# Joined norms between experts and mixer, split products in the merge, tile-wise transposes

## The reference

```python
# first block (one layer)
h = rmsnorm(x, norm1_g); proj = h @ w_in                 # q, k, v of two attentions, two gates
ya, yb = neighbourhood_attention(...), gqa_attention(...)  # each (512, 512)
merged = sigmoid(ga) * (ya @ w_proj_a) + sigmoid(gb) * (yb @ w_proj_b)
x = x + merged @ w_out
x = x + peer(rmsnorm(x, norm2_g), w_q, sub_keys, u, v)   # 16384 experts, 8 heads, top 16
x = rmsnorm(x, norm_f_g)
# second block
h = rmsnorm(x, norm_pre); proj = h @ w_in_2
# causal convolutions, silu, chunked state scan over 16 heads, gated norm, short convolution
mix = concat([y_ssd, y_sc]) @ w_out_2
x = x + rmsnorm(mix, norm_post)
out = x + sigmoid(x @ w_ple_gate) * (p @ w_ple_proj)     # p is (512, 256)
```

## Time and profile before

| | us |
|---|---|
| median of 3 runs | 2385.95 (2381.82 to 2391.55) |
| the profiled execution | 2387.96 |
| its span, first to last instruction | 2386.2 |
| TensorE matmul busy | 2208.9 (93%) |
| VectorE, ScalarE, GpSimd busy | 1517.6, 853.3, 442.6 |
| mean granted TensorE clock | 0.968 |

### The profile page before, as it was taken

One profiled execution on the slowest core, in us unless ns is written; L12 is line 12 of the kernel. 1 busy time (PEld: TensorE's weight loads), 2 busy tenths in 40 slices (PEclk: granted clock), 3 DMA queues, 4 the chain that ended last, 5 costly groups with the idle time before them and its releaser, 6 DMA issues. The chain is left out here.

```text
span 2386.2 us, 29236 instructions
## 1 busy us (share of the span) xinstructions
PE 2208.9 (93%) x11157; PEld 1896.2 (79%) x11157; DVE 1517.6 (64%) x2683; ACT 853.3 (36%) x1419; POOL 442.6 (19%) x306
## 2 busy tenths in 40 slices
PE   7999999798999889889999999999993999989789
PEld 6777666688999888879788888999983798877567
DVE  3546323324999989855888887688886624445643
ACT  3344212222334645763333333333323332222212
POOL 0100000000122010001433333366671000013100
PEclk9999999899999999999999999999996999989899
DMA  5321223212678584668999998799984322210220
GB/s 205 110 84 54 80 106 110 84 36 76 228 249 258 174 253 136 198 217 305 381 378 376 368 378 320 265 354 340 341 284 152 106 89 89 99 43 4 82 101 36
DMA packets 211420, 450.27 MB, mean 189 GB/s; under 512 B 13776, under 2 KB 133584, under 8 KB 204496
## 3 DMA queue, kind: packets, MB, share of 16 engines
q1 hardware_dynamic: 174416, 314.16, 38.0%
q0 software_dynamic: 36864, 134.23, 15.7%
HBM read 403.51 MB, written 44.83 MB: 188 GB/s over the span
## 5 line engine op out<-in xcount | busy, mean ns | idle before, releaser
L1568 PE MATMUL bank<-Vh,Hh 128*128 128x512 f32 x768 | 299.2, 390 | 5.3 <-DVE Hl L1642 5.3
L1570 PE MATMUL bank<-Vh,Hl 128*128 128x512 f32 x768 | 299.5, 390 | 0.0
L1569 PE MATMUL bank<-Vl,Hh 128*128 128x512 f32 x768 | 299.5, 390 | 0.0
L901 PE MATMUL bank<-XH,Ue 128*128 128x384 f32 x672 | 233.2, 347 | 21.6 <-DVE Ue L890 21.6
L939 POOL DMA_INDIRECT ring<-in_v,gidx x128 | 218.6, 1708 | 161.5 <-DVE x_res L951 62.9
L1588 ACT ACTIVATE Vh<-Vr 128x1024 fp32r<-128x1024 f32 x128 | 135.8, 1061 | 303.6 <-PE bank L1570 300.1
L902 PE MATMUL bank<-XL,Ue 128*128 128x384 f32 x672 | 227.6, 339 | 0.0
L903 PE MATMUL bank<-XH,Ue 128*128 128x384 f32 x672 | 227.6, 339 | 0.0
L1637 DVE TENSOR_TENSOR Vl<-Vr,Vh 128x1024 fp32r<-128x1024 f32 x128 | 156.5, 1223 | 54.7 <-ACT Vh L1588 54.7
L939 POOL DMA_INDIRECT ring<-in_u_rows,gidx x92 | 109.8, 1194 | 405.5 <-DVE ghid L944 225.0
L1568 PEld LDWEIGHTS bank<-Vh,Hh 128*128 128x128 f32 x768 | 144.2, 188 | 36.0 <-DVE Hl L1642 7.0
(11 more groups left out here) (360 smaller groups left out, 4890.7 us busy)
## 6 DMA issues: line engine op xcount, KB each, us to landing
Vr<-in_v SPq DMA_DIRECT2D x128, 512.0 KB, 7.2
...
```

Source lines behind the costliest of these rows:

```text
L901: pe.matmul(ps, h[:, k], c.Xh[:, k, 0:DN], start=k == 0, stop=False)
L1568: pe.matmul(ps, Hh[r][:, tok], Vh[r][:, cut], start=p == 0, stop=False)
L1569: pe.matmul(ps, Hh[r][:, tok], Vl[r][:, cut], start=False, stop=False)
L1570: mm = pe.matmul(ps, Hl[r][:, tok], Vh[r][:, cut], start=False, stop=p == PK - 1)
```

## The change

- `transposes_pe` works by token tile: for tile tt it waits for that tile alone and transposes kt 0 to 3; kt 4 to 7 follow as before.
- project: squares of tiles 1 and 3 on VectorE; on both engines the halves of kt 0 to 3, weight piece 0, the halves of kt 4 to 7, pieces 1 and 2.
- merge: the attention outputs are split too (`yh`, `yl`), a third weight piece per m, 3m + 2, holds the projection weights, and L756's matmuls become split ones. Part n of the first half of `w_out` waits for 2(n + 1) merged tiles. `mT` takes the place of `a.y`.
- experts: `due` divides by `work[-LEAD]`. SP also loads `nf`. At the end, tile GT first and then each of the three others as its last matmul is done: VectorE adds the banks and multiplies by `nf` into `c.xn` (in `c.XT`), ScalarE squares both `c.X` and `c.xn`.
- phase_between is gone. mixer_in scales `c.xn` by rr = ((EPS * ss + ss2) / D + EPS^2)^-0.5, which joins both norms, and holds transposes and halves; the residual itself is scaled behind them. Blocks 2 and 3 are loaded only then. Groups 0 to 3 use banks 4 to 7, and group 0 waits k by k.
- scan: at its end the embeddings of the second half, kept in `c.ur` by ScalarE; transposes by tile. mixer_out takes them from there, and TensorE has no `embed` behind the groups.

```diff
...
 def transposes_pe(pe, c, src, n):
-    pe.wait_ge(c.scaled, SCALED[n])
-    for kt in range(KT):
-        if kt >= 4 and n in HALVES:
-            pe.wait_ge(c.xlo, HALVES[n] + kt - 3)
-        elif kt >= 4:
-            pe.wait_ge(c.out_d if kt % 2 else c.out_a, OUT[n] + kt // 2 - 1)
+    for tt in range(TT):
+        pe.wait_ge(c.scaled, SCALED[n] - TT + tt + 1)
+        for kt in range(4):
+            mm = pe.transpose(c.bank[kt][:, tt * P:(tt + 1) * P], src[:, tt, kt * P:(kt + 1) * P], c.ident)
+            if tt == TT - 1:
+                mm.then_inc(c.turned, 1)
+    for kt in range(4, KT):
+        pe.wait_ge(c.xlo, HALVES[n] + kt - 3)
         for tt in range(TT):
             mm = pe.transpose(c.bank[kt % 4][:, tt * P:(tt + 1) * P], src[:, tt, kt * P:(kt + 1) * P], c.ident)
         mm.then_inc(c.turned, 1)
...
-            for tt in range(TT):
+            for tt in range(0, TT, 2):
                 act.wait_ge(c.row_in[tt], 16)
                 act.activation(HN[:, tt], c.X[:, tt], ACT.Square, accum_out=c.ss[:, tt:tt + 1]).then_inc(c.squared, 1)
-            for i in range(3):
-                hi(i)
             act.wait_ge(c.const_in, CONST_FIRST)
-            halves_act(act, c, C_G1, T_FIRST, Xh)
+            halves_act(act, c, C_G1, T_FIRST, Xh, range(4))
+            hi(0)
+            halves_act(act, c, C_G1, T_FIRST, Xh, range(4, KT))
+            hi(1)
+            hi(2)
             for i in range(3, N):
                 hi(i)
...
+            for tt in range(1, TT, 2):
+                dve.wait_ge(c.row_in[tt], 16)
+                dve.tensor_tensor_reduce(HN[:, tt], c.X[:, tt], c.X[:, tt], 1.0, 0.0, ALU.mult, ALU.add, c.ss[:, tt:tt + 1]).then_inc(c.squared, 1)
             dve.wait_ge(c.rooted, N_FIRST + 1)
             for tt in range(TT):
                 dve.wait_ge(c.row_in[tt], 16)
                 dve.tensor_scalar(HN[:, tt], c.X[:, tt], c.rn[:, tt:tt + 1], None, ALU.mult).then_inc(c.scaled, 1)
             dve.wait_ge(c.const_in, CONST_FIRST)
-            for i in range(3):
-                lo(i)
-            halves_dve(dve, c, C_G1, T_FIRST, Xh, Xl)
+            halves_dve(dve, c, C_G1, T_FIRST, Xh, Xl, range(4))
+            lo(0)
+            halves_dve(dve, c, C_G1, T_FIRST, Xh, Xl, range(4, KT))
+            lo(1)
+            lo(2)
...
-        yT, mT = sb("yT", [P, KT, SEQ]), sb("mT", [P, KT, SEQ])
+        yh, yl = (sb(n, [P, KT, SEQ], F32R) for n in ("yTh", "yTl"))
...
             nc, ctx, "m_grp gated halved merged x_grp x_added")
         block = ctx.enter_context(nc.Block())
-        GP = 2 * KT
+        GP = 3 * KT
...
+        def turned(y, kt, dt=None):
...
-                act.wait_ge(grp, 4 * ((i - 2) // 2) + i % 2 + 1)
+                act.wait_ge(grp, 4 * ((i - 2) // 3) + (1, 2, 4)[(i - 2) % 3])
...
                     mm.then_inc(c.turned, 1)
...
-                    pe.wait_ge(c.wlo, W_MERGE + 2 * m + j + 1)
+                    i = 3 * m + j
+                    pe.wait_ge(c.wlo, W_MERGE + i + 1)
                     for k in range(KT):
                         cut = slice(k * P, (k + 1) * P)
...
-                        pe.matmul(bk[j][:], Wh[j][:, cut], Xl[:, k], start=False, stop=False)
-                        mm = pe.matmul(bk[j][:], Wl[j][:, cut], Xh[:, k], start=False, stop=k == KT - 1)
+                        pe.matmul(bk[j][:], Wh[i % 2][:, cut], Xh[:, k], start=k == 0, stop=False)
+                        pe.matmul(bk[j][:], Wh[i % 2][:, cut], Xl[:, k], start=False, stop=False)
+                        mm = pe.matmul(bk[j][:], Wl[i % 2][:, cut], Xh[:, k], start=False, stop=k == KT - 1)
...
                     turn_y()
-                c.wait_w(pe, B_MERGE + m)
+                i = 3 * m + 2
+                pe.wait_ge(c.wlo, W_MERGE + i + 1)
                 for j in range(2):
-                    for k in range(4):
-                        mm = pe.matmul(bk[2 + j][:], w[:, 2 * KT + 4 * j + k], yT[:, 4 * j + k], start=k == 0, stop=k == 3)
+                    pe.wait_ge(c.xlo, S_TURNED + 4 * (j + 1))
+                    for k in range(4 * j, 4 * j + 4):
+                        cut = slice(k * P, (k + 1) * P)
+                        pe.matmul(bk[2 + j][:], Wh[i % 2][:, cut], yh[:, k], start=k % 4 == 0, stop=False)
+                        pe.matmul(bk[2 + j][:], Wh[i % 2][:, cut], yl[:, k], start=False, stop=False)
+                        mm = pe.matmul(bk[2 + j][:], Wl[i % 2][:, cut], yh[:, k], start=False, stop=k % 4 == 3)
                     mm.then_inc(grp, 1)
-            pe.wait_ge(c.xlo, S_MERGED + KT)
             for nh in range(2):
                 for part in range(OP):
                     i = GP + nh * OP + part
                     pe.wait_ge(c.wlo, W_MERGE + i + 1)
+                    if nh == 0:
...
-            transposes_pe(pe, c, yT_as_rows, T_EXPERTS)
+            transposes_pe(pe, c, mT_rows, T_EXPERTS)
...
+            hi(act, 2)
+            for kt in range(KT):
...
+                o, i = turned(yh, kt)
+                act.activation(o, i, ACT.Copy).then_inc(c.xhi, 1)
...
+                    if m + j > 0:
+                        hi(act, 3 * m + 2 + j)
+                if m < KT - 1:
+                    hi(act, 3 * m + 4)
             for k in range(KT):
...
+            hi(act, GP + 1)
...
+            lo(dve, 2)
+            for kt in range(KT):
+                dve.wait_ge(c.xhi, S_TURNED + kt + 1)
+                (o, i), (y_hi, _) = turned(yl, kt), turned(yh, kt, F32)
+                dve.tensor_tensor(o, i, y_hi, ALU.subtract).then_inc(c.xlo, 1)
...
-                lo(dve, 2 * m + 3)
+                if m >= 1:
+                    lo(dve, 3 * m + 2)
+                lo(dve, 3 * m + 3)
...
+                if m < KT - 1:
+                    lo(dve, 3 * m + 4)
...
+            lo(dve, GP + 1)
...
+        nf = c.ar[:].rearrange("p a b -> p (a b)")
...
-        due = [OPS * w // work[-1] for w in work]
+        due = [min(OPS, OPS * w // work[-LEAD]) for w in work]
...
+                    sp.dma_start(nf, t["norm_f"]).then_inc(c.const_in, 16)
...
+                    if p == PK - 1 and tt < DT - 1:
+                        mm.then_inc(tiled, 1)
...
+            act.wait_ge(v_lo, PK)
+            for n, tt in enumerate((GT, *range(DT))):
+                act.wait_ge(final, 3 * n + 1)
+                act.activation(Vr[tt][:], c.X[:, tt], ACT.Square, accum_out=c.ss[:, tt:tt + 1]).then_inc(c.squared, 1)
+                act.wait_ge(final, 3 * n + 2)
+                act.wait_ge(c.squared, N_FINAL * TT + 2 * n + 1)
+                act.activation(Vr[tt][:], c.xn[:, tt], ACT.Square, accum_out=c.ss2[:, tt:tt + 1]).then_inc(c.squared, 1)
...
+            dve.tensor_tensor(c.X[:, GT], c.X[:, GT], acc[:], ALU.add).then_inc(final, 1)
+            dve.wait_ge(c.const_in, CONST_FINAL)
+            for n, tt in enumerate((GT, *range(DT))):
+                if tt < DT - 1:
+                    dve.wait_ge(tiled, tt + 1)
+                elif tt == DT - 1:
+                    dve.wait_ge(summed, PK)
+                if tt < DT:
+                    for nh in range(2):
+                        xs = c.X[:, tt, nh * 512:(nh + 1) * 512]
+                        dve.tensor_tensor(xs, out_bank(tt, nh)[:], xs, ALU.add).then_inc(final, 1)
+                dve.wait_ge(final, 3 * n + 1)
+                dve.tensor_tensor(c.xn[:, tt], c.X[:, tt], nf, ALU.mult).then_inc(final, 1)
...
-def phase_between(c, m_, raw, Xh, Xl):
-
...
-            sp.dma_start(nf[:], t["norm_f"]).then_inc(c.const_in, 16)
-            for b in range(RAW):
-                raw.load(sp, b)
-
-        @block.scalar
-        def _(act):
-            norm_sums(act, c, c.X, HN)
-            act.wait_ge(c.squared, (N_FINAL + 1) * TT)
-            norm_sums(act, c, c.X, HN, xready)
-            halves_act(act, c, C_GPRE, T_PRE, Xh)
...
-        @block.vector
-        def _(dve):
-            dve.wait_ge(c.rooted, N_FINAL + 1)
-            for tt in range(TT):
-                dve.tensor_scalar(c.X[:, tt], c.X[:, tt], c.rn[:, tt:tt + 1], None, ALU.mult).then_inc(xnorm, 1)
-            dve.wait_ge(c.const_in, CONST_FINAL)
-            for tt in range(TT):
-                dve.wait_ge(xnorm, tt + 1)
-                dve.tensor_tensor(c.X[:, tt], c.X[:, tt], nf[:], ALU.mult).then_inc(xready, 1)
-            dve.wait_ge(c.rooted, N_PRE + 1)
-            dve.wait_ge(xready, TT)
-            for tt in range(TT):
-                dve.tensor_scalar(HN[:, tt], c.X[:, tt], c.rn[:, tt:tt + 1], None, ALU.mult).then_inc(c.scaled, 1)
...
-            transposes_pe(pe, c, HN, T_PRE)
...
+            for b in range(2):
+                raw.load(sp, b)
+            sp.wait_ge(c.scaled, SCALED[T_PRE] + TT)
+            for b in range(2, RAW):
+                raw.load(sp, b)
...
+            pool.wait_ge(c.squared, (N_PRE + 1) * TT)
+            pool.tensor_scalar(c.ms2[:], c.ss[:], EPS, 0.0, ALU.mult, ALU.add).then_inc(zero, 1)
+            pool.wait_ge(zero, 1)
```

(61 more changed lines are left out.)

112 lines of the change are left out of this document (42 added, 70 removed).

## The result

The changed kernel takes 2345.83 us (median of 4 runs, 2344.72 to 2346.93) against 2387.76 for the kernel before (4 runs): a ratio of 0.9821, 95% interval 0.9808 to 0.9834. The forecast was 2335.6 with 2327 to 2348. The gain is 42 us where 50 were forecast. The time lies in the range, but outside the 2328 to 2344 of the forecast's own mechanism (0.82): it is in only because the range was stretched over the rivals. It also stands 0.7 us from R1's 2345.1, though the traces refute R1's mechanism, so the range held in part by luck. The profiled execution took 2344.72, its span is 2342.9 (before: 2386.2), so 43.3 us are to be placed.

A forecast was written before the change was run, and what follows sets the result against it. TensorE was taken to set the end, by its streams' length and a few serial chains on other engines at stage borders. Terms summed to 50.4 us off the profiled 2387.96; with the median 2.0 lower, 2335.6 us, range 2327 to 2348.

The forecast's parts named there:

- R1: Rival, expert loop: the DMA queues are full, 371 GB/s is a ceiling, 9.5 us lost, 2345.1 us; chance 0.10.
- (a): Start: half of the squares on VectorE, first four halves ahead of the weight pieces; gain 3.1 us (1.5 to 4.5).
- (b): Merge: 8 plain fp32 matmuls per tile become 24 fp32r, a tile takes 16.32 us; gain 10.2 us (8 to 11.5).
- (c): Merge to out-projection: TensorE's wait for merged halves falls from 3.55 to 1.4 us; gain 2.1 us (0 to 3.5).
- (d): Norm before the experts, transposes by tile: first bank ready after the last tile's first transpose; gain 0.7 us (0 to 1).
- (g): Scan end: embeddings hidden in TensorE's 12.25 us wait, transposes by tile; gain 1.7 us (0.7 to 4).
- (h): Mixer out: transposes by tile gain 1.2 us; last groups every 5.44 us instead of 7.20 gain 6.3 us.
- (e): Expert loop: one more load, norm_f, in SP's queue ahead of u and v loads; loss 1.3 us (0 to 3).
- (f): Seam from experts to mixer: mixer's first group 19.1 us after TensorE's end instead of 42.95; gain 26.4 us (22 to 29).
- R2: Rival, experts: faster gathers hold back v tiles and lengthen every step; slower, 2398 us at 338 GB/s; chance 0.02.
- R3: Rival, merge: the third weight piece comes late, (b) and (c) fall to zero, 2347.9 us; chance 0.05.

The follow-up runs named there:

- plain_y: The changed kernel with the merge's 8 products per tile with the projection weights in plain fp32 again, conversions and waits left as they are: 2350.23 us.
- all_tiles: The changed kernel with transposes that wait for all four token tiles again, everywhere, but keep the new order: 2354.41 us.
- no_seam: The changed kernel with the stage between experts and mixer put back, norm_f loaded there, no tile by tile end of the experts: 2363.14 us, ratio 0.9897.
- shifted: The kernel before with three unused tiles in front of the later buffers, so that these lie 96 bytes higher: 2389.88 us.
- packed: The changed kernel with the norms' six small sums packed into one tile, so later buffers lie at the kernel before's addresses: 2341.47 us, ratio 0.9799.
- packed_both: The changed kernel with the small sums packed and two loads (first three u tiles, mixer's weight block 0) moved ahead: 2333.27 us, ratio 0.9767.
- after_again: The changed kernel once more, with nothing changed: 2346.04 us, ratio 0.9825.
- due_only: The kernel before with the faster dealing of the gathered rows alone: 2380.05 us.

## Why the forecast was right, and where it was not

**The sum.** 50.4 us forecast, 43.3 in the two profiled executions. Most of the difference stands in one row of the table, for which no term existed: from query to the experts stage, 5.4 us lost. The other rows add up to 48.7. These hold errors of both signs, named below, which partly cancel.

**(a) 3.1 us, mis-sized.** In the two profiled executions it is 2.8, but four executions of the old start average 247.8 us up to the merge, nine of the new one 246.7: 1.1 us. The products start at 19.2 to 20.9 us and not 21.1 to 22.0, but the squares on VectorE bring nothing: its scaling ends at 13.7 to 14.7 us, before at 13.7 to 14.5. And the one execution of before that I compared with reached the merge 0.8 to 1.5 us later than its three likes. So 3.1 was nearly three times too high, and the 2.8 of the pair was luck.

**(b) and (c).** The tile takes 16.32 us to the hundredth, and `plain_y` gives 10.1 us for the part. Part 0 starts with no wait and part 1 waits 1.03. On average the two stretches up to query gained 15.5 us (216.9 less 201.4, eight executions) against 13.0 for (b), (c) and (d). The 3.55 us wait became one of 1.03, 2.5 less where 2.1 were forecast. The rest of the surplus is a cost of the old wait that (c) left out: TensorE ran its first products behind it at a low granted clock, 0.50 to 0.65 over 4 us in the four old executions. Kernel before, its repetition, and the changed kernel:

```profile
400.67:404.67 4.00, 4.00 (x12) 3.18 (x13) 0.00 (x0) 0.00 (x0) 0.00 (x0) 0.65 0.78 332
```

```profile
400.45:404.45 4.00, 4.00 (x9) 3.14 (x10) 0.00 (x0) 0.00 (x0) 0.00 (x0) 0.50 0.78 332
```

```profile
385.39:389.39 4.00, 4.00 (x19) 3.33 (x18) 3.68 (x6) 0.26 (x1) 0.00 (x0) 1.00 0.70 221
```

From the out-projection's first product to the norm's last scaled tile it takes 51.2 to 52.8 us in the old executions and 51.1 in the new ones, of which 1.03 is the wait: 1.1 to 2.7 us more behind the old wait, besides its own 3.55.

**(d), (g), (h), transposes by tile.** The terms were of the right size, somewhat high: 2.6 us came of the 3.6. The 8.6 us by time and 12 by marks of `all_tiles` are no price of this part. Of the 6.3 us of (h) 5.5 came: 5.3 from the shorter pitches and 1.2 behind the last, less 1.0 at the first groups, which started at a granted clock of 0.73 where the kernel before had 1.00. So in this pair the clock behind the transposes by tile was lower, and not higher, than behind the old ones.

**(e).** 1.3 us forecast for the load of norm_f and 1.3 measured in the pair, but in part for another reason. With the buffers moved the stretch took 33.4 to 33.8 us with the load and 32.3 without it (`no_seam`, `shifted`); with the buffers as before, 32.6 and 32.9 with it (`packed`, `packed_both`) and 31.3 to 32.4 without. So the load is worth about 1 us and the placement 0.5 to 0.8, and one execution (`after_again`, 36.7) is unexplained. R1 fell at its own test: 380 GB/s with TensorE full. The Trainium skill's figure that I set beside it ("DMA: Bandwidth & Descriptors", Specifications), 358 GB/s per core, is half of what the page gives a stack with two cores; it is passed by the 380 of the trace, where one core ran.

**(f).** The chain was right in each link, 19.1 us to 0.1. What was wrong is whose it is. I booked on the joined norms what `due` gives: 8 us by itself, 14 beside the other edits. In the steps I wrote it as "VectorE has no gathers" and took 2.6 us of waits for it; the 7.1 us by which VectorE ended behind TensorE I never took apart. Those 2.6 us, counted as an earlier end of the loop, did not come: first to last V product took 685.0 us before and 685.5 after, and on average the two kinds differ by less than 0.5. The three short waits for Hl are gone, but the one early in the loop is 4.1 us and not 2.8 (2.1 to 2.8 in three executions with the old dealing and front, 3.5 in `due_only`). The dealing has a part in it; the rest is open. On this stretch the new dealing is worth 1.3 us alone and 1.4 beside the other edits, against the averages of the two kinds.
Left out: "The low clock of the first 8 us after the gap I leave as it is on both sides". The group started at 1.00 here and not at 0.50, which was 2.0 us. It isn't sure to come: in `after_again` and `packed` the group started at 0.54 and 0.51, and the stretch took 290.7 and 290.8 us, as before.

**Query to experts.** Three causes are seen, of which I had none. The placement of the buffers lengthens two waits by 3 us in the sum. The first u tile landed 5.4 us after its issue and not 3.6, so that the first wait was 8.8 and not 7.0; that is 7.0 to 7.1 in four executions with the old front end, 7.0 to 8.9 in eight of the others, and why is open. And which of the short gaps in the stage are answered with a low clock differs from execution to execution: the three gaps of 2.98 us all were in after, two of them before.

**R2 and R3** did not show: V's first to last product took 685.5 us, and no piece of the merge was late.
